# Rounding the next weights after the rounded matmuls of the step before, instead of at that step's end

## The chip, the cores and the metric

The kernel runs on one core of a Trainium2 chip. The metric is the device time of one launch in microseconds (us). The engines that matter are TensorE (PE in the profile; PEld is its loading of the stationary operand), VectorE (DVE), ScalarE (ACT), GpSimd (POOL) and SyncE (SP, which issues the weight transfers).

## The reference

Two layers of an encoder trunk over a sequence of 256 positions and 2048 channels, in float32. Each layer normalises `x`, multiplies it by one wide matrix `w_in`, runs three token mixers on the columns of the product, and puts their gated outputs through three branch matrices and `w_out`:

```
proj = rms_norm(x) @ w_in                      # 21 column chunks of 512 for the mixers, 12 for the merge gates
ya = dilated_attention(qa, ka, va) * silu(a_gate)
yb = banded_window_attention(qb, kb, vb, sink) * silu(b_gate)
yc = hgrn2_bidirectional(c_q, c_ff, c_fb, c_i, c_gate)       # gated linear recurrence, both directions
y  = g0 * (ya @ w_branch_a) + g1 * (yb @ w_branch_b) + g2 * (yc @ w_branch_c)
x  = x + rms_norm(y @ w_out)
```

## The kernel before

**Steps.** All weights of a layer are one stream of 184 tiles of 128 x 2048 float32 (1 MB each). A step `s` is the use of one tile: four blocks of 128 rows by 512 output columns. A chunk of 512 output columns takes 4 steps (16 row blocks), or 1 or 2 for the branch matrices. The layer's body is written for each engine as a loop over `s`, in which an engine does its share of the weight work first and then whatever side work a table of step numbers puts at that `s`. A hardware loop runs the body once for each layer.

**Precision by splitting.** TensorE multiplies in fp32r, which is rounded. So each weight tile is split into a rounded part and a remainder, and each activation likewise. ACT writes the rounded part `w_hi` (L368, two buffers, `s % 2`). DVE (columns 0 to 1279) and POOL (columns 1280 to 2047) write the remainder `w_lo = raw - w_hi` (L371) over the landed tile `raw` in its place (four buffers, `s % 4`). PE then does, for each step, 16 matmuls with `w_hi` (8 against the rounded activations, 8 against their remainders), and after them 8 matmuls with `w_lo`. All add into a PSUM tile `acc` of the chunk.

**Who waits for whom in the weight work.** In iteration `s` of its loop ACT rounds tile `s + 1` (`hi(s + 1)`) as its first action, ahead of its evictions and exponentials. DVE and POOL likewise begin iteration `s` with `lo(s + 1)`, which waits for `hi_ready`. PE waits for `hi_ready` ahead of the 16 matmuls and for `lo_dve` and `lo_pool` ahead of the 8. PE's last matmul of a step adds one to `pe_step`. SP waits for `pe_step` and then refills the `raw` buffer; ACT waits for it before it evicts a finished chunk.

**Between the 16 and the 8 matmuls** PE may call `level_grams(s)`: in the linear recurrence it does there 4 products of 128 x 128 in float32 (8 matmul instructions in the trace) into `side`. The recurrence is done in 4 units of two heads (`REC` = steps 79, 94, 109, 124); each has a preparation on DVE of some 7 steps (reciprocals at L829 and L831, products at L828 to L859) and then 8 levels, one for each step. A level is a ring through four engines: PE's grams; on DVE the copy of them (L872 or L875) and four products (L881 to L884), the last of which adds one to `mixed`; on ACT four exponentials (L696 to L699) that wait for `mixed` and for POOL's `scanned`; on POOL four additions (L515 to L518) that wait for the exponentials. PE's next grams wait for `mixed`. The lines stand in each engine's loop after the weight work of that iteration. In some levels DVE also turns blocks of 32 x 32 (L762), gates a branch (L966) or writes a branch's remainder (L957).

Of the kernel before, what the change touches and what calls it, by code (L numbers as in the profile page):

```python
# [33 lines left out]
CW = 512  # L34
# [90 lines left out]
def build(nc, W, X, CONST, MASKS, LMASKS, PAR, POST, OUT):  # L125
# [4 lines left out]
    with ExitStack() as ctx:  # L130
# [39 lines left out]
        def piece(at, shape, dt=F32):  # L170
# [66 lines left out]
        acc = [ctx.enter_context(nc.psum_tensor(f"acc{i}", [P, MT * CW], F32)) for i in range(2)]  # L237
# [7 lines left out]
        first_landed = [sem(f"first_landed{i}") for i in range(LANDING)]  # L245

        names = """w_landed0 w_landed1 w_landed2 w_landed3 acc_free0 acc_free1 par_landed masks_landed x_landed hi_ready lo_dve lo_pool
            pe_step dve_chain pool_chain x_squared x_rstd_ready sorter_ready rstd_sorted apart_ready x_turned xT_hi_ready xT_ready
            first_hi_ready staged roped turned tanhed scored masked probs probs_turned probs_copied attended
            normed branch_turned branch_hi branch_lo lb_ready rec_prep rec_exp rx_cleared logs_ready mixed grams  # L250
            decays scanned kept rec_out rec_squared rec_rstd_ready rec_y gated summed out_squared out_summed
            out_rstd y_scaled x_new x_new_pool""".split()
        (w_landed0, w_landed1, w_landed2, w_landed3, acc_free0, acc_free1, par_landed, masks_landed, x_landed, hi_ready, lo_dve, lo_pool,
         pe_step, dve_chain, pool_chain, x_squared, x_rstd_ready, sorter_ready, rstd_sorted, apart_ready, x_turned, xT_hi_ready, xT_ready,
         first_hi_ready, staged, roped, turned, tanhed, scored, masked, probs, probs_turned, probs_copied, attended,
         normed, branch_turned, branch_hi, branch_lo, lb_ready, rec_prep, rec_exp, rx_cleared, logs_ready, mixed,
         grams, decays, scanned, kept, rec_out, rec_squared, rec_rstd_ready, rec_y, gated, summed, out_squared,
# [24 lines left out]
        def split_at(s):  # L282

            n = TURN_AT.get(s - 1)
            m = TURN_AT.get(s - 2)
            return m if m in BY_BLOCKS else n if n not in BY_BLOCKS else None

        def lhs(c, k):

            kind = CHUNKS[c][0]  # L290
            if kind == "out":
                return yT_hi[:, k, :], yT_lo[:, k, :]
            if kind == "z_a" or (kind == "z_c" and k < 4):
                return aT_hi[:, k, :], aT_lo[:, k, :]
            if kind == "z_b":
                return bT_hi[:, k, :], bT_lo[:, k, :]
            if kind == "z_c":
                return cT_hi[:, k - 4, :], cT_lo[:, k - 4, :]
            return xT_hi[:, k, :], xT_lo[:, k, :]
# [6 lines left out]
        def apart(v):  # L306

            return v.rearrange("p (t m) -> p m t", m=MT)
# [12 lines left out]
        def key_tiles(u):  # L321

            if u < A_UNITS:
                return [(t * P, 0, t) for t in range(MT)] + [(T + (g - 1) * P, g, u % MT) for g in range(1, NG)]
            return [(257 * i + t * P, i, t) for i in range(4) for t in range(MT)]
# [41 lines left out]
        def w_hi_of(act, s):  # L367
            return act.activation(w_hi[:, s % 2, :], raw[:, s % LANDING, :], ACT.Copy)  # L368
# [62 lines left out]
        def evacuated(eng, c):  # L431

            if c in TURNED:
                eng.wait_ge(staged, TURNED.index(c) + 1)
            else:
                eng.wait_ge(acc_free[c % 2], len([x for x in range(c % 2, c + 1, 2) if x not in TURNED]))

        def layer_body(layer, block):
# [106 lines left out]
            def _(act):  # L545
                def hi(s):

                    if s < LANDING:
                        act.wait_ge(first_landed[s], 16 * (layer + 1))
                    elif s == NSTEPS:  # L550
                        act.wait_ge(first_landed[0], 16 * (layer + 2))
                    else:
                        act.wait_ge(w_landed[s % LANDING], 16 * (s // LANDING))
                    if s >= 2:

                        act.wait_ge(pe_step, s - 1)
                    w_hi_of(act, s).then_inc(hi_ready, 1)

                def scaled(dst, src, func, scale, done=None):
# [6 lines left out]
                for s in range(NSTEPS + 3):  # L566
                    if s < NSTEPS:
                        hi(s + 1)
# [15 lines left out]
                    c = ENDS.get(s - 1)  # L584
                    if c is not None:
                        kind, i, _ = CHUNKS[c]
                        act.wait_ge(pe_step, s)
                        if c in TURNED:
                            n = TURNED.index(c)
# [27 lines left out]
                        elif kind.startswith("merge"):  # L617
                            n = MERGES.index(c)
# [15 lines left out]
                    c = ENDS.get(s - 5)  # L634
# [3 lines left out]
                    for u, s0 in enumerate(UNITS):  # L638
                        if s == s0 + 2:
# [5 lines left out]
                            else:  # L645

                                for i in range(4):
                                    v = scores[:, 257 * i:257 * i + 257]
                                    ins = act.activation(v, v, ACT.Exp, bias=nmax[:, b, i:i + 1], scale=SCALE,
                                                         accum_out=dens[:, b, i:i + 1])  # L650
                                    if i == 3:
                                        ins.then_inc(probs, 1)
                        if s == s0 + 3:
# [3 lines left out]
                            n = P * len(key_tiles(u))  # L657
                            act.activation(probsT[:, 0:n], side[1][:, 0:n], ACT.Copy).then_inc(probs_copied, 1)
                    n = split_at(s)
                    if n is not None:  # L660
# [3 lines left out]
                        if n == 0:  # L664

                            for m in range(MT):
                                ins = act.activation(dst.rearrange("p i (t m) -> p i m t", m=MT)[:, :, m],
                                                     src[:, :, m * P:(m + 1) * P], ACT.Copy, scale=0.5)
# [3 lines left out]
                        else:  # L672
                            for i in range(blocks):
                                ins = act.activation(dst[:, i], src[:, i], ACT.Copy, scale=gain[:, i:i + 1])
                            ins.then_inc(branch_hi, 1)
                    for u in range(4):
# [23 lines left out]
                        if d == FIRST_LEVEL + 9:  # L700
                            act.wait_ge(rec_out, u + 1)
                            for i in range(4):
                                ins = act.activation(wide[:, i * P:(i + 1) * P], side[1][:, i * P:(i + 1) * P], ACT.Square,
                                                     scale=0.5, accum_out=rec_sq[:, i:i + 1])
# [339 lines left out]
            def _(pe):  # L1044
                def mm(out, a, b, start=True, stop=True):
                    return pe.matmul(out, a, b, start=start, stop=stop)  # L1046

                def stream(s, between):
                    c, q = STEPS[s]
                    kind, i, k = CHUNKS[c]  # L1050
                    tile = (lambda v, m: apart(v)[:, m]) if kind in ("gate_a", "v_a") else (lambda v, m: v[:, m * P:(m + 1) * P])
                    if q == 0 and c >= 2:

                        evacuated(pe, c - 2)
                    if c == 0 and q:
                        pe.wait_ge(xT_ready, 2 * q)
                    if kind[:2] == "z_" and i == 0 and q == 0:
                        pe.wait_ge(branch_lo, {"z_a": 1, "z_b": 3, "z_c": 7}[kind])
                    if kind == "out" and i == 0:
                        pe.wait_ge(branch_lo, 8 + q)  # L1060
                    if s:
                        pe.wait_ge(hi_ready, s)
                    for t in range(QK):
                        w = w_hi[:, s % 2, t * CW:(t + 1) * CW]
                        for n, part in enumerate(lhs(c, QK * q + t)):
                            for m in range(MT):
                                mm(acc[c % 2][:, m * CW:(m + 1) * CW], tile(part, m), w,
                                   start=(q == 0 and t == 0 and n == 0), stop=False)
                    between()
                    if s:  # L1070
                        pe.wait_ge(lo_dve, s)
                        pe.wait_ge(lo_pool, s)
                    for t in range(QK):
                        w = w_lo[:, s % LANDING, t * CW:(t + 1) * CW]
                        part = lhs(c, QK * q + t)[0]
                        for m in range(MT):
                            ins = mm(acc[c % 2][:, m * CW:(m + 1) * CW], tile(part, m), w, start=False,
                                     stop=(q == k // QK - 1 and t == QK - 1))
                    ins.then_inc(pe_step, 1)
# [23 lines left out]

                for s in range(NSTEPS):
                    stream(s, lambda: level_grams(s))
                    if s == APART_AT:

                        pe.wait_ge(x_rstd_ready, 1)
                        pe.wait_ge(sorter_ready, 1)
                        for m in range(MT):  # L1110
                            ins = mm(side[1][:, 4 * m:4 * m + 4], wide[:, m * P:(m + 1) * P], small[:, 22:26])
                        ins.then_inc(rstd_sorted, 1)
                    for u, s0 in enumerate(UNITS):
                        q, k, m = unit(u)
                        if s == s0:
# [9 lines left out]
                            for i in range(len(q)):  # L1125
# [6 lines left out]
                                ins = mm(out, q[i], k[i])  # L1132
                            ins.then_inc(scored, 1)
                        if s == s0 + 2:
# [4 lines left out]
                            for n, (at, _, _) in enumerate(key_tiles(u)):  # L1139
                                ins = pe.transpose(side[1][:, n * P:(n + 1) * P], scores[:, at:at + P], ident)  # L1140
                            ins.then_inc(probs_turned, 1)
                        if s == s0 + 3:
# [6 lines left out]
                            for n, (_, i, t) in enumerate(tiles_):  # L1149
                                w = probsT[:, n * P:(n + 1) * P]  # L1150
                                if u < A_UNITS:
                                    h = u // MT
                                    ins = mm(side[1][:, 0:P], w, va[:, i, t, h * HD:(h + 1) * HD],
                                             start=(n == 0), stop=(n == len(tiles_) - 1))
                                else:
                                    kv = (u - A_UNITS) // MT
                                    ins = mm(side[1][:, i * P:(i + 1) * P], w, vb[:, t, kv * HD:(kv + 1) * HD],
                                             start=(t == 0), stop=(t == MT - 1))
                            ins.then_inc(attended, 1)
                    for u in range(4):  # L1160
# [3 lines left out]
                        if d == FIRST_LEVEL + 8:  # L1164
# [4 lines left out]
                            for h in range(2):  # L1169
                                for tt in range(MT):  # L1170
# [3 lines left out]
                                    ins = mm(o, S_off[:, h * MT + 1 - tt], v[:, 1 - tt, (j + h) * HD:(j + h + 1) * HD],  # L1174
                                             start=False)
                            ins.then_inc(rec_out, 1)
                    n = TURN_AT.get(s)
                    if n is not None and n not in BY_BLOCKS:
# [4 lines left out]
                        for i in range(blocks):  # L1183
                            for m in range(MT):
                                ins = pe.transpose(ps[:, i * T + m * P:i * T + (m + 1) * P],
                                                   src[:, m, i * P:(i + 1) * P], ident)
# [98 lines left out]
```

## Time and profile before

| what | value |
|---|---|
| time, median of 3 runs | 2307.32 us (2306.56 to 2308.26) |
| span of the profiled execution | 2304.9 us |
| outside the span, against the median | 2.4 us |
| PE busy | 2233.6 us, 97% of the span |
| DVE / POOL / ACT busy | 1606.6 / 1319.2 / 1034.5 us |
| mean granted TensorE clock | 0.991 |

The profile gives no time of its own for the profiled execution beside its span, so the span is set against the median of the runs. A row of a timeline reads: start, length, engine, line, operation, tile written and tiles read, how many instructions were merged into the row, and in brackets the idle time of the engine just before it with what ended it. A row of merged instructions has one length for all of them.

### The profile page before, as it was taken

The page shows a single profiled execution, that of the slowest core. Times are in us where ns is not written, and L with a number is a line of the kernel's source. Part 1 is how long each engine was busy: PE and PEld are TensorE (multiplying, and loading weights), DVE is VectorE, ACT ScalarE, POOL GpSimd, SP SyncE. Part 2 cuts the span into 40 slices and gives each one's busy share as a digit, 9 for nine tenths or more (in the row PEclk, how much of TensorE's full clock was granted, in tenths as well). Part 3 has the DMA queues.
Part 4 walks back from the last instruction along what each step waited for, and adds up shares of the span by engine and source line. Part 5 has one row for each costly group of instructions (what it writes and reads, how often), then busy time and mean ns, then how long its engine had stood idle before and what let it go on. Part 6 is the DMA issues. An engine that isn't in the chain of part 4 may idle for free. (4 is left out here: it accounts for less than half of the span.)

```text
span 2304.9 us, 27183 instructions
## 1 busy us (share of the span) xinstructions
PE 2233.6 (97%) x10272; PEld 1843.1 (80%) x10272; DVE 1606.6 (70%) x2139; ACT 1034.5 (45%) x1112; POOL 1319.2 (57%) x658
## 2 busy tenths in 40 slices
PE   8999999998999889999989999999989998899999
PEld 6888888886888778888778888888868887788887
DVE  4773358789998897554357723587899899974634
ACT  5434344444455444344444434444455554444343
POOL 4555544446586567666545555443464865676655
PEclk9999999999999999999999999999999999999999
DMA  7555544453444344655555554443535444446555
GB/s 281 197 186 188 178 161 168 147 183 129 178 160 174 131 162 159 243 192 192 192 180 199 183 190 175 153 176 138 191 130 181 160 169 146 146 165 243 196 183 201
DMA packets 61676, 409.31 MB, mean 178 GB/s; under 512 B 6880, under 2 KB 7008, under 8 KB 13664
## 3 DMA queue, kind: packets, MB, share of 16 engines
q1 hardware_dynamic: 61248, 407.32, 49.5%
q8 instruction: 84, 1.38, 0.2%
q14 instruction: 56, 0.46, 0.1%
q10 hardware_dynamic: 288, 0.16, 0.0%
HBM read 401.16 MB, written 6.29 MB: 177 GB/s over the span
## 5 line engine op out<-in xcount | busy, mean ns | idle before, releaser
L371 POOL TENSOR_TENSOR w_lo<-raw,w_hi 128x768 fp32r<-128x768 f32 x369 | 1034.5, 2804 | 901.6 <-ACT w_hi L368 894.6
L368 ACT ACTIVATE w_hi<-raw 128x2048 fp32r<-128x2048 f32 x369 | 709.3, 1922 | 1102.4 <-PE acc L1046 1086.4
L371 DVE TENSOR_TENSOR w_lo<-raw,w_hi 128x1280 fp32r<-128x1280 f32 x369 | 617.6, 1675 | 644.7 <-ACT w_hi L368 641.7
L1046 PE MATMUL acc<-w_hi,xT_hi 128*128 128x512 f32 x2368 | 742.4, 395 | 6.2 <-issue 4.7
L1046 PE MATMUL acc<-w_hi,xT_lo 128*128 128x512 f32 x2368 | 733.9, 391 | 0.0
L1046 PE MATMUL acc<-w_lo,xT_hi 128*128 128x512 f32 x2368 | 609.5, 400 | 4.1 <-DVE w_lo L371 4.0
L1046 PEld LDWEIGHTS acc<-w_lo,xT_hi 128*128 128x128 f32 x2368 | 445.0, 190 | 104.1 <-DVE w_lo L371 6.3
L1046 PEld LDWEIGHTS acc<-w_hi,xT_lo 128*128 128x128 f32 x2368 | 447.0, 189 | 97.1
L1046 PEld LDWEIGHTS acc<-w_hi,xT_hi 128*128 128x128 f32 x2368 | 443.2, 189 | 100.2 <-issue 6.8
L762 DVE STREAM_TRANSPOSE arena<-stage 32x256 f32<-32x256 f32 (+1 forms) x480 | 204.9, 427 | 7.2
L1046 PE MATMUL side<-arena 128*128 128x128 f32 (+1 forms) x864 | 131.3, 297 | 45.7 <-DVE arena L884 44.0
L1046 PEld LDWEIGHTS side<-arena 128*128 128x128 f32 x864 | 119.7, 198 | 64.0 <-DVE arena L884 53.7
L515 POOL TENSOR_TENSOR arena<-arena 128x256 f32<-128x256 f32 x56 | 69.8, 1246 | 59.1 <-ACT arena L699 59.1
L762 DVE STREAM_TRANSPOSE arena<-arena 32x256 f32<-32x256 f32 x192 | 83.7, 436 | 2.9
L1046 PE MATMUL acc<-w_hi,yT_hi 128*128 128x512 f32 x256 | 79.8, 393 | 0.0
L1046 PE MATMUL acc<-w_hi,yT_lo 128*128 128x512 f32 x256 | 79.4, 391 | 0.0
L562 ACT ACTIVATE stage<-acc,small 128x512 f32<-128x512 f32 (+1 forms) x108 | 66.7, 669 | 19.2 <-DVE arena L762 19.2
L1046 PE MATMUL acc<-w_lo,yT_hi 128*128 128x512 f32 x256 | 65.0, 395 | 0.0
L884 DVE TENSOR_TENSOR arena<-arena 128x256 f32<-128x256 f32 x64 | 64.3, 1005 | 0.0
L516 POOL TENSOR_TENSOR arena<-arena 128x256 f32<-128x256 f32 x56 | 59.7, 1066 | 0.0
L696 ACT ACTIVATE arena<-arena 128x256 f32<-128x256 f32 x64 | 27.0, 422 | 71.0 <-DVE arena L884 40.2
L1046 PEld LDWEIGHTS acc<-w_lo,yT_hi 128*128 128x128 f32 x256 | 48.0, 188 | 11.4
(142 smaller groups left out, 1853.8 us busy)
## 6 DMA issues: line engine op xcount, KB each, us to landing
raw<-w_stream SPq DMA_DIRECT2D x372, 1024.0 KB, 4.8
x_out<-arena SPq DMA_DIRECT2D x12, 512.0 KB, 4.0
arena<-x_out SPq DMA_DIRECT2D x8, 512.0 KB, 5.8
arena<-x_in SPq DMA_DIRECT2D x4, 512.0 KB, 8.5
wide<-post_in SPq DMA_DIRECT2D x2, 1024.0 KB, 6.8
arena<-masks_in SPq DMA_DIRECT2D x2, 768.0 KB, 7.4
arena<-lmasks_in SPq DMA_DIRECT2D x2, 448.0 KB, 8.5
const<-const_in ACTq DMA_DIRECT2D x1, 128.0 KB, 4.6
```

The lines of the kernel that those rows point to most:

```text
L368: return act.activation(w_hi[:, s % 2, :], raw[:, s % LANDING, :], ACT.Copy)
L371: return eng.tensor_tensor(w_lo[:, s % LANDING, cols], raw[:, s % LANDING, cols], w_hi[:, s % 2, cols].bitcast(F32), ALU.subtract)
L515: pool.tensor_tensor(rx_lo, rx_lo, last(pf_up), ALU.add)
L516: link(pool.tensor_tensor(rb_up, rb_up, head(pb_lo), ALU.add))
L562: ins = act.activation(dst[:, m], src[:, m], func, scale=scale[:, m:m + 1])
L696: act.activation(ef_up, halves(PI[:, 0], l)[1], ACT.Exp)
L762: ins = dve.transpose(dst[ch].rearrange("p h (m t) -> p m h t", m=MT)[:, :, :, pos], src[pos].rearrange("p m (h d) -> p m h d", d=HD)[:, : ...
L884: dve.tensor_tensor(q_lo, halves(q, l)[0], eb_lo, ALU.mult).then_inc(mixed, 1)
L1046: return pe.matmul(out, a, b, start=start, stop=stop)
```

## The change

`hi(s)` waited, from `s = 2` on, for `pe_step >= s - 1`: PE had to be through all 24 matmuls of step `s - 2`, the last reader of the `w_hi` buffer that is written anew. Now PE has a further semaphore `hi_used`, to which the last of the 16 `w_hi` matmuls of each step adds one. `hi(s)` waits for it instead, and from `s = 3` on also for the remainders of step `s - 2` by DVE and POOL, since these read the same `w_hi` buffer.

```
@@ ACT, in hi(s)
                     if s >= 2:
 
-                        act.wait_ge(pe_step, s - 1)
+                        act.wait_ge(hi_used, s - 1)
+                    if s >= 3:
+                        act.wait_ge(lo_dve, s - 2)
+                        act.wait_ge(lo_pool, s - 2)
                     w_hi_of(act, s).then_inc(hi_ready, 1)
@@ PE, in stream(s, between)
                             for m in range(MT):
-                                mm(acc[c % 2][:, m * CW:(m + 1) * CW], tile(part, m), w,
-                                   start=(q == 0 and t == 0 and n == 0), stop=False)
+                                ins = mm(acc[c % 2][:, m * CW:(m + 1) * CW], tile(part, m), w,
+                                         start=(q == 0 and t == 0 and n == 0), stop=False)
+                    ins.then_inc(hi_used, 1)
                     between()
```

No instruction is added, removed or put elsewhere in an engine's order; PE has 1754 rows and ACT 490 in both kernels. Only waits differ. On ACT, around the first levels of the first unit of the recurrence, the program reads before:

```order
L368 ACTIVATE w_hi<-raw 128x2048 [waits pe_step,w_landed0]
L696 ACTIVATE arena<-arena 128x128x2 [waits scanned,mixed]
L697 ACTIVATE arena<-arena 128x128x2
L698 ACTIVATE arena<-arena 128x128x2
L699 ACTIVATE arena<-arena 128x128x2
L368 ACTIVATE w_hi<-raw 128x2048 [waits pe_step,w_landed1]
```

and with the change, where the lines are numbered three higher:

```order
L368 ACTIVATE w_hi<-raw 128x2048 [waits lo_dve,lo_pool,hi_used,w_landed0]
L699 ACTIVATE arena<-arena 128x128x2 [waits scanned,mixed]
L700 ACTIVATE arena<-arena 128x128x2
L701 ACTIVATE arena<-arena 128x128x2
L702 ACTIVATE arena<-arena 128x128x2
L368 ACTIVATE w_hi<-raw 128x2048 [waits lo_dve,lo_pool,hi_used,w_landed1]
```

The rounding stands at the same place in ACT's order, ahead of the level's four exponentials; what it waits for has changed.

## Rows read from the trace of the kernel before

**Rows 1.** Span and mean granted clock; then the page's busy times.

```profile
core 0: 2304.9 us, clock 0.991
...
PE 2233.6 (97%) x10272; PEld 1843.1 (80%) x10272; DVE 1606.6 (70%) x2139; ACT 1034.5 (45%) x1112; POOL 1319.2 (57%) x658
```

**Rows 2.** The page's group of roundings: busy, mean, idle before and its releaser.

```profile
L368 ACT ACTIVATE w_hi<-raw 128x2048 fp32r<-128x2048 f32 x369 | 709.3, 1922 | 1102.4 <-PE acc L1046 1086.4
```

**Rows 3.** Waits of PE over the whole span: total, times, longest.

```profile
PE side L1046 <- DVE arena L884: 44.0, 23, 4.3
...
PE acc L1046 <- DVE w_lo L371: 4.0, 2, 2.0
```

**Rows 4.** Stretches of the first layer: busy by engine, then granted clock, DMA.

```profile
500.00:576.00 76.00, 66.81 (x296) 54.07 (x295) 71.16 (x82) 35.78 (x41) 47.37 (x32) 0.96 0.42 146
...
804.00:840.00 36.00, 33.98 (x141) 27.05 (x140) 32.87 (x42) 15.04 (x10) 17.29 (x9) 0.95 0.46 169
```

**Rows 5.** Timeline of PE at the first unit: a plain step, then grams.

```profile
500.32 2.03 PE L1046 MATMUL acc<-w_lo,xT_hi 128*128 128x512 f32 x8
...
533.54 1.05 PE L1046 MATMUL side<-arena 128*128 128x128 f32 x8
...
542.54 1.16 PE L1046 MATMUL side<-arena 128*128 128x128 f32 x8 [2.44 <-DVE arena L884]
...
569.31 2.08 PE L1046 MATMUL side<-arena 128*128 128x128 f32 x8 [3.43 <-DVE arena L884]
```

**Rows 6.** Timeline of ACT and DVE ahead of the first unit's levels.

```profile
502.45 1.92 ACT L368 ACTIVATE w_hi<-raw 128x2048 fp32r<-128x2048 f32 x1 [0.64 <-PE acc L1046]
...
504.41 1.49 DVE L371 TENSOR_TENSOR w_lo<-raw,w_hi 128x1280 fp32r<-128x1280 f32 x1 [2.81 <-ACT w_hi L368]
...
537.92 0.68 DVE L872 COPY arena<-side 128x512 f32<-128x512 f32 x1
```

**Rows 7.** Timelines of POOL and DVE: last products of levels and remainders.

```profile
540.40 1.80 POOL L371 TENSOR_TENSOR w_lo<-raw,w_hi 128x768 fp32r<-128x768 f32 x1 [0.18 <-POOL arena L518]
540.43 2.05 DVE L884 TENSOR_TENSOR arena<-arena 128x256 f32<-128x256 f32 x1
...
548.64 2.06 DVE L884 TENSOR_TENSOR arena<-arena 128x256 f32<-128x256 f32 x1
...
677.38 0.41 DVE L884 TENSOR_TENSOR arena<-arena 128x256 f32<-128x256 f32 x1
677.74 3.14 POOL L371 TENSOR_TENSOR w_lo<-raw,w_hi 128x768 fp32r<-128x768 f32 x1 [0.57 <-ACT w_hi L368]
...
1917.17 2.06 DVE L884 TENSOR_TENSOR arena<-arena 128x256 f32<-128x256 f32 x1
```

**Rows 8.** The second unit: DVE at its first grams.

```profile
640.21 0.69 DVE L872 COPY arena<-side 128x512 f32<-128x512 f32 x1 [1.04 <-PE side L1046]
```

**Rows 9.** The third unit: PE's first two grams, DVE's copy.

```profile
733.25 1.05 PE L1046 MATMUL side<-arena 128*128 128x128 f32 x8
...
734.99 0.68 DVE L872 COPY arena<-side 128x512 f32<-128x512 f32 x1
...
739.65 1.05 PE L1046 MATMUL side<-arena 128*128 128x128 f32 x8
```

**Rows 10.** The fourth unit's preparation and first levels: ACT, DVE, PE.

```profile
804.68 1.92 ACT L368 ACTIVATE w_hi<-raw 128x2048 fp32r<-128x2048 f32 x1 [2.61 <-PE acc L1046]
...
806.63 1.49 DVE L371 TENSOR_TENSOR w_lo<-raw,w_hi 128x1280 fp32r<-128x1280 f32 x1 [5.88 <-ACT w_hi L368]
...
824.03 3.00 DVE L371 TENSOR_TENSOR w_lo<-raw,w_hi 128x1280 fp32r<-128x1280 f32 x1
...
827.08 3.08 PE L1046 MATMUL acc<-w_lo,xT_hi 128*128 128x512 f32 x8 [2.00 <-DVE w_lo L371]
...
847.59 1.16 PE L1046 MATMUL side<-arena 128*128 128x128 f32 x8 [1.23 <-DVE arena L884]
```

**Rows 11.** The second layer: the first wait for grams.

```profile
1689.14 1.16 PE L1046 MATMUL side<-arena 128*128 128x128 f32 x8 [2.44 <-DVE arena L884]
```

More of the change, by code:

```diff
@@ L247, in build @@
         names = """w_landed0 w_landed1 w_landed2 w_landed3 acc_free0 acc_free1 par_landed masks_landed x_landed hi_ready lo_dve lo_pool
-            pe_step dve_chain pool_chain x_squared x_rstd_ready sorter_ready rstd_sorted apart_ready x_turned xT_hi_ready xT_ready
+            hi_used pe_step dve_chain pool_chain x_squared x_rstd_ready sorter_ready rstd_sorted apart_ready x_turned xT_hi_ready xT_ready
             first_hi_ready staged roped turned tanhed scored masked probs probs_turned probs_copied attended
@@ L253, in build @@
         (w_landed0, w_landed1, w_landed2, w_landed3, acc_free0, acc_free1, par_landed, masks_landed, x_landed, hi_ready, lo_dve, lo_pool,
-         pe_step, dve_chain, pool_chain, x_squared, x_rstd_ready, sorter_ready, rstd_sorted, apart_ready, x_turned, xT_hi_ready, xT_ready,
+         hi_used, pe_step, dve_chain, pool_chain, x_squared, x_rstd_ready, sorter_ready, rstd_sorted, apart_ready, x_turned, xT_hi_ready, xT_ready,
          first_hi_ready, staged, roped, turned, tanhed, scored, masked, probs, probs_turned, probs_copied, attended,
```

## The prediction

> **What bounds the kernel now.** I read the busy times first. PE is busy for 2233.6 of 2304.9 us [rows 1], so all that any change of waits can win is 71.3 us of PE's idle time and what the clock gives back: (1 - 0.991) x 2304.9 = 20.7 us. Next I read the groups. ACT's 1102 us of waiting for PE ahead of its roundings [rows 2] look like the target, but they are idle time of an engine that is ahead: PE needs 6.4 us for a step with grams (733.25 to 739.65 [rows 9]), so about 5.5 us for one without, and the rounding takes 1.92 us of that. Shortening this wait wins nothing there. What counts is the list of PE's own waits: 44.0 us in 23 waits ahead of grams, for DVE's last product of a level, and 4.0 us in 2 waits for DVE's remainders [rows 3]. The other 23 us of idle time lie at the start, at the border of the layers and at the end, where PE waits for `x` or for the new `x`; the change doesn't touch them, since the wait that is left out there has long been over.
>
> So the question is whether DVE reaches a unit's levels earlier. The timeline answers it unit by unit. The reader should look for the last row of DVE ahead of a wait of PE that says "idle, ended by w_hi": from there on DVE works without a pause, and its lateness at the grams is fixed by when that rounding came.
>
> **What the change does to the times.** PE's 8 matmuls with `w_lo` take 2.03 us [rows 5]. In steps without grams ACT may now round 2.03 us earlier, in steps with grams about 2.9 us earlier (grams 1.05 us with a small overlap). Evictions stand behind the rounding in ACT's order but wait for the step's end themselves; with the rounding (1.92 us [rows 2]) done by then they also start about 1.9 us earlier. So ACT, DVE and POOL all shift by about 2 us against PE, with the same phase between them. No wait becomes later: PE's end of step `s - 2`, for which ACT waited, already implied that the remainders of that step had been made. What does not shift is DVE's copy of grams, which follows PE. The new increments and the two more waits cost nothing that I can price above zero: ACT stands idle for 1102 us ahead of its roundings [rows 2], and PE issues no instruction more. If that cover were gone, 184 waits in a layer at an estimated few hundredths of a us would be under 10 us on ACT alone.
>
> **Unit by unit, first layer.**
> First unit. DVE waits 2.81 us at 504.41 for the rounding that ACT began at 502.45, after 0.64 us of waiting for PE [rows 6]. ACT itself is 2 us earlier there, since what holds it before is an eviction and DVE's first six operations of the unit, both of which shift. From 504.41 DVE has no pause until the first levels. It copies the first grams at 537.92, while PE had ended them at 533.54 + 1.05 = 534.59 [rows 5, 6]: 3.3 us late, so the whole 2.03 us can be used. PE's first wait, 2.44 us at 542.54, falls to about 0.4. The next three waits (the last is 3.43 us at 569.31 [rows 5]) stay: there DVE is the bound by its own work, 8.2 us for a level with remainders, copy, products and turned blocks (last product at 540.43 and at 548.64 [rows 7]), against 6.4 of PE. Gain 2.0.
> Second unit. DVE waits 1.04 us for PE's grams at 640.21 [rows 8]. It is early already; a lead is lost at that point. Gain 0, between -1 and +1 by where POOL's remainders fall.
> Third unit. The copy begins at 734.99, PE's grams ended at 733.25 + 1.05 = 734.30 [rows 9]. Of the lead 0.7 us can be used. Gain 0.7.
> Fourth unit. DVE waits 5.88 us at 806.63 for the rounding of 804.68, which waited 2.61 us for PE [rows 10]; ACT can be 2.03 earlier. The chain goes without a pause to the remainders at 824.03, which end at 827.03; PE needs them at 827.08 - 2.00 = 825.08. With the lead they end at 825.0, and the wait of 2.00 us goes, and with it the slow clock behind it (the 8 matmuls took 3.08 instead of 2.03 us). But this is not a gain of 2.0 + 1.7 (the stretch's clock of 0.95 over 36 us [rows 4]): DVE goes on without a pause into the levels, where PE waits for it again at 847.59 [rows 10]. PE comes there earlier and waits longer, 3 us instead of 1.23. What remains is the shift of DVE's chain. Gain 2.0. That wait is what is late next.
>
> Together 4.7 us for a layer. The second layer has the same waits at the same places (2.44 us at 1689.14 for 2.44 at 542.54 [rows 5, 11]), so 9.4 us.
>
> **What it may cost.** DVE and POOL hinder each other. The last product takes 0.41 us alone and 2.05 us where POOL's remainders started 0.03 us ahead of it; and POOL's take 3.14 us instead of 1.80 where DVE was first [rows 7]. Both kernels have one such meeting in nearly every level. In before, 13 of the 64 last products take over 2 us (the first at 540.43, the last at 1917.17 [rows 7]). With the rounding earlier, POOL no longer pauses for it behind its additions: at 677.74 it had waited 0.57 us [rows 7], and would now start at 677.35, just ahead of the product at 677.38. Such pauses of POOL inside the levels are about 7 in a layer. At most of them DVE's product is over or was blocked already; where it isn't, 1.64 us are added to a product that PE needs about 1.3 us later, so 0.3 us of waiting. I take 0.5 us for a layer, between 0 and 7 x 1.64 = 11.5. The sum is 9.4 - 1.0 = 8.4 us. Against the span: 2304.9 - 8.4 = 2296.5, and with the 2.4 us outside 2298.9 us.
>
> The Trainium skill ("SBUF — State Buffer", section "Who interferes with whom") says that a DVE instruction with two inputs in SBUF contends with a GpSimd instruction that reads SBUF, and that whichever issues first blocks the other fully. By it each meeting has a loser, and moving POOL's start ahead of DVE's makes DVE the loser; that is the last rival below, which is priced from rows 7. The two pairs of durations above agree with it. Its rule that issue order decides would make the cost 11.5 us in a layer if each of the 7 pauses turned into a block on PE's path, and 0.5 by the margins of the rows; I go by the margins.
>
> **The rivals.**
> *The lead is lost (no change).* A level's ring is PE, DVE, PE; roundings are not in it. If DVE's preparation doesn't keep its 2 us, because an eviction, `mixed` or POOL's meetings hold it the gain is 0 to 3 us: 2304 to 2308. For it: the waits 2 to 4 of the first unit and those of the second are DVE's work alone. Against it: the phases of the three engines stay alike. 0.22.
> *More than the lead.* The clock was 0.96 over 76 us and 0.95 over 36 [rows 4], which is worth 3.0 and 1.8 us, and over the span 20.7. A shorter first wait, or POOL's additions being earlier by 2.9 us in each level, may spare one or two such falls in each layer: 6 to 13 us more, 2286 to 2292. Against it: the long waits of 3.4 us and more that stand before the falls are not shortened by a lead. 0.15.
> *POOL goes first (slower).* POOL's remainders, freed from the rounding, start ahead of DVE's last product in most levels. 64 levels less the 13 where this is so already are 51. With 1.64 us each less the 1.1 us by which DVE is early in a level without other work, each adds 0.5 us of waiting: 26 us, less the gain of 9.4: 17 slower, 2324 us. It decides from about 19 levels on. Against it: in most of the levels POOL comes from its additions without waiting for a rounding (0.18 us behind L518, as at 540.40 [rows 7]), and there the change moves nothing. 0.10.
>
> **How the numbers follow.** My forecast, the lead kept in three units, has 0.53, with its own range of 2294 to 2303: gains of 2.0 + 0 + 0.7 + 2.0 with the second unit at plus or minus 1, and the meetings between 0 and 2 us a layer. For 8 in 10 I reach over the gains with one fall of the clock in each layer spared, to 2287, and above over the case of no change, to 2308. 0.2% of the time is 4.6 us, about what a measurement can tell from no change; faster begins below 2302.7. The forecast's case gives 0.50 to faster and 0.03 to same; the case of more 0.15 to faster; the lost lead 0.03 to faster, 0.18 to same and 0.01 to slower; POOL first 0.02 to same and 0.08 to slower. Together 0.68, 0.23 and 0.09.
>
> **What would show it.** Right: ACT's roundings start at the end of the `w_hi` matmuls and end before the step does; DVE's wait for the rounding ahead of the first unit ends 2 us earlier against PE; PE's first wait of the first unit is under 1 us, the later three are as before; the wait for `w_lo` (4.0 us) is gone, and the one at the fourth unit's first products is longer; PE's waits for L884 total 36 to 40 us. Wrong: the number of last products over 2 us well above 13, or PE's waits spread over levels that had none; or a total of waits far below 36, or a mean clock above 0.994, for then the falls of the clock were spared too.

## The result and the profile after

The changed kernel takes 2316.78 us (median of 5 runs, 2312.11 to 2318.49), the one before 2307.43 us (5 runs beside them, 2306.56 to 2308.26). The ratio is 1.0036, with a 95% interval of 1.0024 to 1.0049: slower, by about 9 us. The forecast was 8.4 us faster.

The page of the changed kernel gives its span and busy times:

```profile
span 2310.2 us, 27547 instructions
...
PE 2235.9 (97%) x10272; PEld 1841.2 (80%) x10272; DVE 1639.0 (71%) x2139; ACT 1033.4 (45%) x1112; POOL 1295.9 (56%) x658
```

The profiled execution took 2312.11 us and was the fastest of the five; its span is 5.3 us over that of before [rows 1]. DVE, with the same 2139 instructions, is busy for 1639.0 instead of 1606.6 us. That is the first line to stop at: no instruction was added, so the same instructions have become 32 us longer. They wait inside their own busy time.

PE's waits over the whole span of the changed kernel (total, times, longest; L887 and L890 here are L884 and L887 of before):

```profile
PE side L1049 <- DVE arena L887: 40.3, 29, 4.2
...
PE side L1049 <- DVE arena L890: 7.9, 6, 2.6
...
PE acc L1049 <- DVE w_lo L371: 3.8, 4, 1.4
```

Against [rows 3] the waits are shorter and more: 29 for last products instead of 23, and 6 new ones for L890, DVE's copy of a unit's last grams.

Most of DVE's extra time lies in the groups of its four products of a level (busy us, mean ns of one). Before:

```profile
L884 DVE TENSOR_TENSOR arena<-arena 128x256 f32<-128x256 f32 x64 | 64.3, 1005 | 0.0
L882 DVE TENSOR_TENSOR arena<-arena 128x256 f32<-128x256 f32 x64 | 53.5, 836 | 0.0
L883 DVE TENSOR_TENSOR arena<-arena 128x256 f32<-128x256 f32 x64 | 51.9, 811 | 0.0
L881 DVE TENSOR_TENSOR arena<-arena 128x256 f32<-128x256 f32 x64 | 41.2, 643 | 6.7 <-ACT arena L699 6.6
```

and with the change:

```profile
L887 DVE TENSOR_TENSOR arena<-arena 128x256 f32<-128x256 f32 x64 | 75.4, 1179 | 0.0
L886 DVE TENSOR_TENSOR arena<-arena 128x256 f32<-128x256 f32 x64 | 61.8, 965 | 0.0
L885 DVE TENSOR_TENSOR arena<-arena 128x256 f32<-128x256 f32 x64 | 52.0, 812 | 0.0
L884 DVE TENSOR_TENSOR arena<-arena 128x256 f32<-128x256 f32 x64 | 46.3, 724 | 6.8 <-ACT arena L702 6.7
```

The sum rises from 210.9 to 235.5 us, by 24.6. Counted in the timeline, 13 of the 256 products took over 1.9 us before, all of them last products (L884). Now 28 do: 21 last products (L887) and 7 third products (L886), of which none did before. I call these products blocked. Most of the rise is theirs. That 15 more by 1.64 us each (2.05 - 0.41 [rows 7]) give just 24.6 us is partly chance: an unblocked product took 0.4 to 1.6 us by what POOL did beside it, and the first product of a level (L881, now L884) rose by 5.1 us with none over 1.9.

**Where PE gained and lost.** The start of like rows of PE in both traces shows it:

| PE at | before, us | after, us | after - before |
|---|---|---|---|
| layer 1, unit 1, first grams | 533.54 | 532.43 | -1.1 |
| unit 1, fifth grams | 569.31 | 566.42 | -2.9 |
| unit 1, outputs (16 matmuls) | 600.54 | 600.37 | -0.2 |
| unit 3, first grams | 733.25 | 733.03 | -0.2 |
| unit 3, outputs | 797.01 | 793.51 | -3.5 |
| unit 4, first grams | 839.80 | 834.57 | -5.2 |
| unit 4, outputs | 899.78 | 899.63 | -0.2 |
| layer 2, first products of `arena` into `side` | 1396.69 | 1398.85 | +2.2 |
| layer 2, unit 1, first grams | 1680.14 | 1681.13 | +1.0 |
| unit 1, outputs | 1745.77 | 1750.72 | +5.0 |
| unit 4, first grams | 1983.04 | 1984.83 | +1.8 |
| unit 4, outputs | 2044.73 | 2049.94 | +5.2 |

The lead is there: it wins on the way into the first and the fourth unit of the first layer, and inside the third unit. It is given back inside the levels of the first and of the fourth unit, in both layers. Not all of that is new. In the fourth unit of the first layer PE waits 4.14 us at the second grams instead of 1.23: 2.9 of the 5.1 us that are given back there are the longer wait of the forecast.

And not all of the loss lies in the levels. Between the fourth unit and the second layer 2.3 us are lost, at the border of the layers. Before, and then with the change:

```profile
1154.68 1.97 PE L347 MATMUL side<-const,arena 128*128 128x128 f32 x16 [0.23 <-DVE arena L1036]
```

```profile
1154.65 3.26 PE L347 MATMUL side<-const,arena 128*128 128x128 f32 x16 [0.23 <-DVE arena L1039]
```

The matmuls are the same and so is the wait ahead of them; the mean granted clock from 1154 to 1174 us is 0.83 before and 0.74 with the change. No row ties this to the change: in the 14 traces of this case the stretch from the fourth unit's outputs to the second layer's first row of the table is 496.9 to 500.4 us long, and the kernel before has the shortest. So the 5.3 us between the two spans are, by PE's rows, almost wholly 2.6 us more of waiting in the recurrence (40.3 + 7.9 instead of 44.0, and 1.6 for L762) and 2.3 us more of busy time (2235.9 - 2233.6), as much as the border lost.

The first unit in the changed kernel, on PE's timeline:

```profile
532.43 1.05 PE L1049 MATMUL side<-arena 128*128 128x128 f32 x8
...
539.64 1.16 PE L1049 MATMUL side<-arena 128*128 128x128 f32 x8 [0.64 <-DVE arena L887]
547.87 1.16 PE L1049 MATMUL side<-arena 128*128 128x128 f32 x8 [1.55 <-DVE arena L887]
...
566.42 1.16 PE L1049 MATMUL side<-arena 128*128 128x128 f32 x8 [3.43 <-DVE arena L887]
...
574.40 1.16 PE L1049 MATMUL side<-arena 128*128 128x128 f32 x8 [1.33 <-DVE arena L887]
...
582.33 1.16 PE L1049 MATMUL side<-arena 128*128 128x128 f32 x8 [1.28 <-DVE arena L887]
...
600.37 2.05 PE L1049 MATMUL side<-arena 128*128 128x128 f32 x16 [0.90 <-DVE arena L890]
```

The first wait fell from 2.44 [rows 5] to 0.64 us, the others up to 3.43 stayed, as forecast. But before, no wait came behind that of 3.43 us in this unit; now there are five more (two of them, 0.47 and 0.29 us, are not shown). The two timelines side by side say why. Before, in the fifth level:

```profile
575.14 0.41 DVE L884 TENSOR_TENSOR arena<-arena 128x256 f32<-128x256 f32 x1
...
576.89 1.85 POOL L371 TENSOR_TENSOR w_lo<-raw,w_hi 128x768 fp32r<-128x768 f32 x1 [1.96 <-ACT w_hi L368]
```

and with the change, in the same level and the next:

```profile
572.24 1.82 POOL L371 TENSOR_TENSOR w_lo<-raw,w_hi 128x768 fp32r<-128x768 f32 x1 [0.18 <-POOL arena L518]
572.27 2.07 DVE L887 TENSOR_TENSOR arena<-arena 128x256 f32<-128x256 f32 x1
...
580.18 1.81 POOL L371 TENSOR_TENSOR w_lo<-raw,w_hi 128x768 fp32r<-128x768 f32 x1 [0.18 <-POOL arena L518]
580.20 2.07 DVE L887 TENSOR_TENSOR arena<-arena 128x256 f32<-128x256 f32 x1
```

Before, POOL stood for 1.96 us waiting for a rounding that stood waiting for PE, and DVE's product ran in 0.41 us. Now the rounding is long done, POOL starts 0.18 us behind its last addition, 0.03 us ahead of the product, and the product takes 2.07 us. PE waits for it.

A blocked product does not always cost PE time. Behind all 13 of the kernel before PE waits for the next grams; behind only 13 of the 28 with the change does it wait more than 0.1 us. Of the other 15, 14 lie in the second, third and fourth units.

The clock hides a part here. The same wait of 3.43 us stands in both traces, but PE's level behind it (569.31 to 578.60) is 9.29 us of busy time before, at a mean granted clock of 0.67, and 6.65 us with the change (566.42 to 574.40), at 1.00. In the second layer both kernels have this fall (0.81 and 0.80), and the first unit loses 4.0 us there, instead of 0.9 in the first layer.

The end of the fourth unit shows a second form of the same:

```profile
895.22 2.41 POOL L536 TENSOR_TENSOR arena<-arena,stage 128x1024 f32<-128x1024 f32 x1 [1.82 <-DVE stage L969]
895.29 3.68 DVE L371 TENSOR_TENSOR w_lo<-raw,w_hi 128x1280 fp32r<-128x1280 f32 x1 [0.16 <-DVE stage L969]
...
899.63 2.05 PE L1049 MATMUL side<-arena 128*128 128x128 f32 x16 [2.00 <-DVE arena L890]
```

POOL, ahead with its remainders, takes its addition of a branch (L536) just before DVE's remainders, and the copy of grams behind these comes 2.0 us late for PE.

### The profile page after: what moved, and what is told of

The parts are those of the page before. It is cut to its first block and busy times, and to the rows that moved or that the text cites. A ratio compares the mean times of both kernels' runs of the same rounds, so it can differ in the third digit from the quotient of the medians.

```text
span 2310.2 us, 27547 instructions
## 1 busy us (share of the span) xinstructions
PE 2235.9 (97%) x10272; PEld 1841.2 (80%) x10272; DVE 1639.0 (71%) x2139; ACT 1033.4 (45%) x1112; POOL 1295.9 (56%) x658
## 5 line engine op out<-in xcount | busy, mean ns | idle before, releaser
L371 POOL TENSOR_TENSOR w_lo<-raw,w_hi 128x768 fp32r<-128x768 f32 x369 | 1023.3, 2773 | 869.9 <-ACT w_hi L368 859.4
L1049 PE MATMUL side<-arena 128*128 128x128 f32 (+1 forms) x864 | 130.9, 296 | 48.3 <-DVE arena L887 40.3
L515 POOL TENSOR_TENSOR arena<-arena 128x256 f32<-128x256 f32 x56 | 60.6, 1083 | 93.3 <-ACT arena L702 93.3
L887 DVE TENSOR_TENSOR arena<-arena 128x256 f32<-128x256 f32 x64 | 75.4, 1179 | 0.0
L886 DVE TENSOR_TENSOR arena<-arena 128x256 f32<-128x256 f32 x64 | 61.8, 965 | 0.0
L516 POOL TENSOR_TENSOR arena<-arena 128x256 f32<-128x256 f32 x56 | 60.9, 1087 | 0.0
```

The lines of the kernel that those rows point to most:

```text
L371: return eng.tensor_tensor(w_lo[:, s % LANDING, cols], raw[:, s % LANDING, cols], w_hi[:, s % 2, cols].bitcast(F32), ALU.subtract)
L515: pool.tensor_tensor(rx_lo, rx_lo, last(pf_up), ALU.add)
L516: link(pool.tensor_tensor(rb_up, rb_up, head(pb_lo), ALU.add))
L886: dve.tensor_tensor(q_up, halves(q, l)[1], ef_up, ALU.mult)
L887: dve.tensor_tensor(q_lo, halves(q, l)[0], eb_lo, ALU.mult).then_inc(mixed, 1)
```

## The experiments

Theory 1 is that of the last rival: **POOL goes first**. Theory 2: the falls of TensorE's clock lie elsewhere by chance. Theory 3: the waits and increments that were added cost time themselves. "Level steps" are the steps of the 8 levels of each unit and the one behind them. Each time below is the median of 4 to 7 runs; each ratio is to runs of the kernel before on the same chip, which took 2305.5 to 2308.6 us.

| kernel | us | ratio (95%) | products over 1.9 us |
|---|---|---|---|
| before | 2307.4 | 1 | 13 |
| the change | 2316.8 | 1.0036 (1.0024 to 1.0049) | 28 |
| change, POOL behind the last product | 2279.5 | 0.9882 (0.9867 to 0.9898) | 0 |
| change outside level steps only | 2300.4 | 0.9967 (0.9956 to 0.9979) | 10 |
| change in level steps only | 2322.7 | 1.0073 (1.0059 to 1.0086) | 22 |
| before, POOL behind the last product | 2283.0 | 0.9899 (0.9884 to 0.9914) | 0 |
| change, POOL writes zeros | 2262.1 | 0.9806 (0.9790 to 0.9822) | 2 |
| before, POOL writes zeros | 2266.7 | 0.9824 (0.9808 to 0.9841) | 1 |
| change, POOL waits for the step's end | 2294.3 | 0.9951 (0.9934 to 0.9967) | 4 |
| change, DVE waits for the step's end | 2314.1 | 1.0038 (1.0024 to 1.0052) | 28 |
| POOL behind, change outside level steps only | 2280.9 | 0.9886 (0.9869 to 0.9902) | 0 |
| change, POOL behind, columns 1024 and 1024 | 2287.5 | 0.9912 (0.9895 to 0.9928) | 10 |
| before, one wait more that is always met | 2288.6 | 0.9924 (0.9907 to 0.9940) | 4 |
| change, one wait more that is always met | 2292.0 | 0.9938 (0.9922 to 0.9955) | 7 |

**1. The change, POOL behind the last product.**

```
 def lo(s):      # POOL
+    for u in range(4):
+        l = s - 1 - REC[u] - FIRST_LEVEL
+        if 0 <= l <= LEVELS:
+            pool.wait_ge(mixed, (LEVELS + 1) * u + l + 1)
     pool.wait_ge(hi_ready, s)
```

> The changed kernel, and in the levels of the recurrence POOL's remainders also wait for the last product of the level before (the semaphore mixed). Theory 1, POOL goes first: the change loses because POOL's remainders now start just ahead of DVE's products in the levels; with them held behind the product the slow-down goes and the lead shows, 2292 to 2303 us, and products over 1.5 us fall from 30 to under 8. Theory 2, the falls of TensorE's clock: they lie elsewhere by chance, and holding POOL changes nothing sure: 2310 to 2320 us. Theory 3, the added waits and increments cost time by themselves: 2312 to 2320 us.

2279.5 us: 37 us below the change and 27 below the kernel before, far under what I gave. No product is over 1.9 us. The groups of the four products in this kernel:

```profile
L889 DVE TENSOR_TENSOR arena<-arena 128x256 f32<-128x256 f32 x64 | 52.2, 816 | 0.0
L890 DVE TENSOR_TENSOR arena<-arena 128x256 f32<-128x256 f32 x64 | 50.5, 789 | 0.0
L888 DVE TENSOR_TENSOR arena<-arena 128x256 f32<-128x256 f32 x64 | 45.3, 708 | 6.8 <-ACT arena L706 6.7
L891 DVE TENSOR_TENSOR arena<-arena 128x256 f32<-128x256 f32 x64 | 42.7, 667 | 0.0
```

The last product fell from a mean of 1179 to 667 ns. The meeting is not only the change's loss; the kernel before paid for it too.

**2. and 3. The change outside or inside the level steps only.**

```
+in_levels = any(FIRST_LEVEL <= s - 1 - r <= FIRST_LEVEL + LEVELS for r in REC)
+if s >= 2 and in_levels:            # the third kernel: not in_levels
+    act.wait_ge(pe_step, s - 1)
+elif s >= 2:
     act.wait_ge(hi_used, s - 1)     # and lo_dve, lo_pool from s = 3 on
```

> The early rounding in all steps but those of the levels (and the step behind them), where the wait is the old one. Theory 1: POOL is held back in the levels as before, the lead into the units is kept: 2298 to 2304 us. Theory 2: anything between 2304 and 2318. Theory 3: about the share of steps outside the levels, some 60 per cent of the loss, 2312 us.

> The early rounding only in the steps of the levels (and the step behind them). Theory 1: all of the loss and none of the lead: 2316 to 2324 us. Theory 2: between 2304 and 2318. Theory 3: some 40 per cent of the loss, 2311 us.

-6.5 us outside (2300.4 - 2306.9) and +15.8 us inside (2322.7 - 2306.9). The two add up to +9.3, which is what the whole change cost. So the early rounding is a gain of 6.5 us on the way into the units and a loss of 16 in the levels. Theory 3 fell: the added waits run in 148 of the 184 steps of a layer in the second kernel (the level steps are 36, a fifth and not the 40 per cent of the expectation), and it is faster. Theory 2 had all four of these kernels between 2304 and 2320 us; they lie at 2279.5, 2300.4, 2322.7 and, below, 2283.0. So the clock by itself is not the cause. In the third kernel PE's waits read:

```profile
PE side L1051 <- DVE arena L889: 46.4, 30, 4.3
...
PE side L1051 <- DVE arena L892: 5.7, 4, 2.0
```

**4. The kernel before, with POOL behind the last product** (the lines of the first experiment in the kernel before).

> The kernel before, with POOL's remainders in the levels held behind the last product of the level before. Theory 1: the 13 products over 2 us go, a part of it on PE's path: 2300 to 2306 us. Theories 2 and 3: no change, 2307.

2283.0 us. My price of the meetings was far too low again: 24 us, not 1 to 7. With POOL held, the early rounding is worth 3.5 us (2279.5 against 2283.0). The clock is a part of the 24 us: between the profiled executions before (2304.9 us) and here (2278.2), PE's waits in the recurrence fell by 20.3 us (from 45.6 to 25.3) and its busy time by 6.9 (2233.6 to 2226.7), with the mean granted clock at 0.995 instead of 0.991.

**5. and 6. POOL's remainders read nothing in the level steps.** They are replaced by zeros; this part of the remainders is left out of the result.

```
     pool.wait_ge(hi_ready, s)
+    if in_levels:
+        pool.memset(w_lo[:, s % LANDING, POOL_COLS].bitcast(F32), 0.0).then_inc(lo_pool, 1)
+    else:
         w_lo_of(pool, s, POOL_COLS).then_inc(lo_pool, 1)
```

> The changed kernel, in which POOL in the level steps only writes zeros into its columns of the remainder, in place of reading the raw and the rounded weights (that part of the remainders is left out of the result). Theory 1, POOL's reads go ahead of DVE's products: without them the change has nothing to lose, and is faster than its partner without the early rounding, by 3 to 9 us; about 2268 to 2282 us. If the loss came from anything else in the levels (ACT's order, the waits, the clock), the pair keeps the distance of 9 us: this one 2285 to 2292.

> The kernel before with the same zeros written by POOL in the level steps. Theory 1: DVE's products are hindered by POOL's additions alone, 2274 to 2286 us, and 3 to 9 us above the changed kernel with zeros. Otherwise some 9 us below it.

2262.1 and 2266.7 us. Without POOL's subtractions in the level steps the sign of the change turns: it is a gain of 4.7 us. PE's waits for last products, with the change and zeros:

```profile
PE side L1052 <- DVE arena L890: 8.6, 7, 2.8
```

and before with zeros:

```profile
PE side L1049 <- DVE arena L887: 12.3, 10, 2.7
```

So whatever else the change does in the levels costs nothing that shows; what it costs hangs on POOL's remainders. These kernels were expected a little higher. The 40 us by which the second is under the kernel before are no price of the meetings alone: a write of zeros took 0.74 us on POOL where the subtraction took 1.80 or more, so POOL's additions also came earlier. 24 us are got back by order alone in the fourth experiment. The three products still over 1.9 us in this pair (2.65 to 2.70 us) began 0.03 us behind a POOL addition of 128x1024, which reads, and none behind the zeros: in the changed kernel with zeros 88 products began while POOL wrote zeros, and each took 0.41 to 0.43 us. So it is POOL's reads that block.

**7. and 8. Who must not be early.** In the changed kernel POOL's remainders, or DVE's, wait in the level steps for the step's end as well.

```
+    if s >= 2 and in_levels:
+        pool.wait_ge(pe_step, s - 1)      # the eighth kernel: dve.wait_ge(pe_step, s - 1)
```

> The changed kernel, in which POOL's remainders in the level steps also wait for pe_step, the end of the step for which the rounding waited before. POOL then starts at most 1.9 us (a rounding) earlier than before the change. Theory 1: most of the loss inside the levels is undone, the lead stays: 2302 to 2311 us, products over 1.9 us between 10 and 20. If DVE's or ACT's earlier start were the cause: 2314 to 2320.

> The changed kernel, in which DVE's remainders in the level steps wait for pe_step, and POOL's do not. Theory 1: POOL goes first as in the changed kernel, 2314 to 2324 us, products over 1.9 us about 28. If DVE's own earlier remainders were the cause: 2300 to 2309.

POOL held: 2294.3 us. DVE held: 2314.1 us, and 28 long products, like the change. So it is POOL's start and not DVE's. But the seventh lies 8 us under the lower end that I gave, and 12 us under the kernel before, though POOL waits here for the same step's end as the rounding did before the change. Its timeline of the first unit shows the reason:

```profile
540.32 0.41 DVE L889 TENSOR_TENSOR arena<-arena 128x256 f32<-128x256 f32 x1
...
540.36 2.08 POOL L371 TENSOR_TENSOR w_lo<-raw,w_hi 128x768 fp32r<-128x768 f32 x1 [0.24 <-POOL arena L520]
```

PE had ended its step at about 538.1, so POOL was not held here at all. It starts 0.24 us behind its addition instead of 0.18 [rows 7], since it has one more wait to pass. That puts it 0.04 us behind the product instead of 0.03 ahead.

**11. and 12. One more wait that is always met.** This tests that reading. Each waits for a value of `pe_step` that `hi_ready` already implies.

```
+    if s >= 2 and in_levels:
+        pool.wait_ge(pe_step, s - 1)      # kernel before; in the changed one s >= 3 and s - 2
```

> The kernel before, with one more wait on POOL ahead of its remainders in the level steps, for a value of pe_step that the rounding has already waited for: it is met whenever hi_ready is, and only lengthens POOL's queue, by some 0.06 us by the run in which POOL waited for pe_step. In the kernel before POOL starts 0.02 to 0.03 us ahead of DVE's last product (540.40 to 540.43). If who goes first is settled by such a margin: products over 1.9 us fall from 13 to under 6, and 2282 to 2296 us. If what counts is that POOL is really held: 2305 to 2309.

> The changed kernel with one more wait on POOL in the level steps, for pe_step of two steps before, which is met whenever hi_ready is. If the margin of some hundredths decides: 2285 to 2298 us, near the run in which POOL waited for the step's end (2294). If that run gained by holding POOL to the step's end: 2312 to 2320.

2288.6 and 2292.0 us: 17 us under the kernel before and 25 under the changed one, by a wait that holds nothing back. In the first of them, the second level:

```profile
545.93 0.41 DVE L886 TENSOR_TENSOR arena<-arena 128x256 f32<-128x256 f32 x1
...
545.97 2.06 POOL L371 TENSOR_TENSOR w_lo<-raw,w_hi 128x768 fp32r<-128x768 f32 x1 [0.24 <-POOL arena L520]
```

Some hundredths of a us settle who goes first.

**9. and 10. With POOL held: is the early rounding inside good for anything, and is DVE's share right?** The ninth has the edits of the first and the second experiment. The tenth is the first with 1024 columns for each engine in the level steps.

> POOL's remainders held behind the last product as in the first experiment, but the rounding early only outside the level steps. If inside the levels the early rounding costs only by letting POOL go first, it is now neither good nor bad there: 2277 to 2281 us, like the kernel with the early rounding everywhere and POOL held (2279.5). If it has a cost of its own inside the levels: below 2275. If it has a gain of its own there: 2282 to 2286.

> The changed kernel with POOL held behind the last product, and in the level steps 1024 columns of the remainders for each of DVE and POOL, in place of 1280 and 768. If DVE's own work bounds the levels now, 0.3 us less for each level on DVE where it waits for nothing: 2270 to 2278 us. If POOL's longer remainders (0.6 us more) and the additions behind them become the bound of the ring: 2282 to 2300 us.

2280.9 us (ratio 0.9886, against 0.9882 in the first experiment): no difference can be told, so inside the levels the early rounding has no effect of its own. 2287.5 us for the new split: slower than the first by 0.3%. POOL's longer remainders now run into the next level: 10 of its first products (L888) take over 1.9 us. ACT's first exponential shows who bounds the ring then, in the tenth kernel:

```profile
L703 ACT ACTIVATE arena<-arena 128x256 f32<-128x256 f32 x64 | 27.1, 423 | 152.3 <-POOLq L523 80.5 <-DVE arena L891 68.5 <-DVE arena L866 3.1
```

and in the first:

```profile
L703 ACT ACTIVATE arena<-arena 128x256 f32<-128x256 f32 x64 | 27.1, 423 | 134.5 <-DVE arena L891 88.4 <-POOLq L523 44.0 <-DVE arena L866 2.0
```

Its waits for POOL's additions grow from 44.0 to 80.5 us. The first and the ninth kernel are the best of those that compute all.

## Why the prediction was wrong

**What bounds the kernel** was read rightly: PE's waits for last products of levels. That roundings are not in the ring is confirmed by the ninth experiment.

**"Gain 2.0, 0, 0.7, 2.0" (the lead).** The mechanism is right. In the changed trace the rounding starts at 499.56, at the end of the `w_hi` matmuls, and DVE's wait ends at 501.52, which is 1.9 us earlier against PE than before. The size was too high: 9.4 us forecast, 6.5 measured in the kernel with the change outside the level steps alone, 4.7 in the pair with zeros. It even holds a gain that I had ruled out when I wrote that the change doesn't touch PE's other idle time: two waits of 0.8 us for turned blocks (L762), one in each layer ahead of the recurrence, are gone. One part of it is the fourth unit, where I let the wait for `w_lo` go. It did not: 3.8 us in 4 waits are left of 4.0 in 2. PE's rows there:

```profile
821.78 2.13 PE L1049 MATMUL acc<-w_lo,xT_hi 128*128 128x512 f32 x8 [0.50 <-DVE w_lo L371]
828.95 2.13 PE L1049 MATMUL acc<-w_lo,bT_hi 128*128 128x512 f32 x8 [1.39 <-DVE w_lo L371]
```

"The same phase between them" was not quite true: a product group in the preparation took 3.16 us where it took 1.57 before, because POOL's remainders now met it and not DVE's remainders.

**"I take 0.5 us for a layer" (the meetings).** This is the step that failed. It was 1.0 us in the sum; the early rounding in the level steps alone cost 15.8 us net (the third kernel), and only by letting POOL go first, since with POOL held it cost nothing (the ninth). Two things were wrong in it. I counted only the 7 pauses of POOL in a layer and judged each by the place at which DVE stood in the trace of before. But once the first pause goes, the levels behind it run at other phases, so margins read from the old trace don't hold; 15 more products were blocked, 7 of them third products, which I had not looked at.

And I took the 1.1 to 1.3 us by which DVE is early as a cushion for each. In the first unit DVE has no cushion, since its other work fills the level: the new blocks at 572.27 and 580.20 are followed by waits of PE of 1.33 and 1.28 us, not 0.3. At the end of the fourth unit it is DVE's remainders that are blocked (3.68 us at 895.29), and PE waits 2.00 us, a form that the sum did not have. Where DVE has its cushion I was right: the one pause that I worked out, at 677.35, did turn (in the changed trace the product at 676.67 takes 2.10 us), and PE does not wait there.

**"DVE is the bound by its own work, 8.2 us for a level"** in the first unit was wrong too. Of these 8.2 us, 1.64 were the blocked product. In the fourth experiment, which takes the blocks out of the kernel before, the same two last products are 6.85 us apart (538.68 and 545.53), and PE's wait there is under 0.1 us. I had explained as work what was in part a wait inside an instruction.

**The rivals.** "POOL goes first" had the right mechanism, 0.10 of the chance and 2324 us. It came out at 2316.8 because its gain and its loss were both smaller (6.5 and 15.8 us instead of 9.4 and 26), and fewer products turned (15 instead of 51). "It decides from about 19 levels on" was too high: it priced each at 0.5 us, and where the levels have no cushion it was 1.3. "More than the lead" was not seen as a gain of the change, but its falls of the clock are real: one of 2.6 us was spared in the first unit of the first layer and not in that of the second, and no row shows why. The rule of the Trainium skill ("SBUF — State Buffer", section "Who interferes with whom"), that issue order decides who is blocked, is what the runs show: 0.41 us for a product that starts 0.04 us ahead of POOL, 2.07 for one that starts 0.03 us behind. The same section says that an instruction of GpSimd which only writes SBUF does not contend with a DVE instruction of two inputs. The pair with zeros agrees: 0.41 to 0.43 us for the 88 products that began during such a write. Weighing that rule by the margins of the old trace, and not by whether its order could change, was the error. (The 3.14 us of POOL in [rows 7] were read beside the product at 677.38; in the trace POOL stood there behind DVE's remainders, which began at 677.72, 0.02 us ahead of it.)

**What stays open.** The trace explains 5.3 of the 9.3 us, since the profiled run was the fastest of five, and 2.3 of these are the clock at the border. The changed kernel's runs spread over 6.4 us, those of before over 1.7. By their medians experiments 2 and 3 place the whole loss in the level steps, but what differs from run to run no trace here shows. Nor is there a price for a blocked product: the third kernel has 9 more than the kernel before and the changed one 15 more, for about the same loss inside the levels. Where they lie counts.

## What to carry to other kernels

Where two engines hinder each other, an earlier start of the one that isn't on the path can cost more than it gives: look in the timeline for pairs that start within some hundredths of a us of each other, and ask what wait kept the loser back until now. Order such a pair by a semaphore (here POOL's remainders behind `mixed`); that was worth 24 us on the old kernel and 37 on the changed one. Before calling an engine bound by its own work, compare the longest and the shortest duration of the same instruction.

## What the runs showed of the hardware

A wait that is already met delayed POOL by 0.06 us: it began its remainders 0.24 us behind its addition instead of 0.18, in the seventh, eleventh and twelfth kernel alike. By that alone the kernel before became 0.8% faster (2288.6 us), and its blocked products fell from 13 to 4.

A DVE product of 128x256 with both inputs in SBUF took 0.41 us alone, mostly 0.8 to 1.1 next to POOL's additions of the same size, and 2.05 to 2.10 behind POOL's 128x768. With a POOL instruction that only wrote (the zeros) in place of the 128x768, the 88 products that began beside it in the changed kernel took 0.41 to 0.43 us.

The same matmuls behind the same waits did not run at the same granted clock in two traces: 16 products of 128x128 took 1.97 us in one and 3.26 in the other, in stretches with a mean granted clock of 0.83 and 0.74.
